# A mixture-of-experts layer on one core: three weight buffers become one ring of 20 slots

## The reference

```python
def moe_ffn(h, w_router, b_router, w_gate_up, b_gate_up, w_down, b_down):
    logits = (h @ w_router + b_router).astype(jnp.float32)
    top_v, top_e = lax.top_k(logits, TOP_K)                    # TOP_K = 4
    gate = jax.nn.softmax(top_v, axis=-1)
    ...                                                        # tokens sorted by expert, in blocks
    def expert_block(args):
        xblk, e = args
        gu = xblk @ w_gate_up[e] + b_gate_up[e]                # w_gate_up[e]: 1024 x 2048
        g = jnp.minimum(gu[:, :D_FF], SWIGLU_LIMIT)
        u = jnp.clip(gu[:, D_FF:], -SWIGLU_LIMIT, SWIGLU_LIMIT)
        hid = g * jax.nn.sigmoid(SWIGLU_ALPHA * g) * (u + 1.0)
        return hid @ w_down[e] + b_down[e]                     # w_down[e]: 1024 x 1024
    ...                                                        # weighted by gate, added per token
```

## Time and profile before

| | |
|---|---|
| timed runs, median | 1397.04 us |
| profiled execution | 1398.15 us |
| its span | 1396.1 us |
| TensorE busy (matmul) | 1076.9 us, 77% |
| TensorE weight load busy | 511.5 us, 37% |
| DVE / ACT / GpSimd busy | 426.2 / 222.2 / 117.9 us |
| moved by DMA | 472.35 MB, mean 338 GB/s |

### The profile page before, as it was taken

How to read it: one execution, slowest core, us unless ns; L and a number is a source line. 1 busy time by engine, 2 the same in 40 slices (tenths; PEclk the granted TensorE clock), 3 DMA queues, 4 the chain that set the end, 5 groups by cost and what they waited for, 6 DMA issues and landing times.

```text
span 1396.1 us, 25367 instructions
## 1 busy us (share of the span) xinstructions
PE 1076.9 (77%) x10234; PEld 511.5 (37%) x10235; DVE 426.2 (31%) x989; ACT 222.2 (16%) x428; POOL 117.9 (8%) x46
## 2 busy tenths in 40 slices
PE   3599999978796668666988997997666589666875
PEld 1367677764332223112433342342221134212322
DVE  1596787953221112111322221221111123111214
ACT  2121132113111011000121211121100011100112
POOL 0154334600000000000000000000000000000001
PEclk9899999985989889888999999999878899887987
DMA  9887956618899999999669989819999994999991
GB/s 314 260 312 249 337 213 196 247 69 354 338 417 417 419 418 418 419 416 417 288 259 417 418 348 379 342 48 418 418 418 419 418 384 170 418 418 419 416 417 71
DMA packets 111142, 472.35 MB, mean 338 GB/s; under 512 B 10736, under 2 KB 14448, under 8 KB 78224
## 3 DMA queue, kind: packets, MB, share of 16 engines
q1 hardware_dynamic: 108832, 469.03, 84.1%
q10 hardware_dynamic: 2288, 3.02, 0.9%
HBM read 470.98 MB, written 1.05 MB: 338 GB/s over the span
## 4 chain that ended last, share of the span: by engine, by line
PE 40%; DMA 36%; SPq 15%; DVE 4%; issue 3%; ACT 1%; POOL 0%; ACTq 0%; DVEq 0%
DMA down<-in_w_down_dram 17%; DMA gate_up<-in_w_gate_up_dram 16%; PE bank L1567 13%; PE bank L1234 9%; SPq L355 8%; PE bank L1602 8%; SPq L348 4%; PE bank L1537 3%; PE bank L1523 2%; DVE gate_up_r L721 2%; DMA gate_up<-in_w_ada_dram 2%; DMA gate_up<-in_w_in_dram 1%; PE bank L1256 1%; DMA gate_up<-in_w_o_b_dram 1%; ACT mod L695 1%
## 5 line engine op out<-in xcount | busy, mean ns | idle before, releaser
L1567 PE MATMUL bank<-gate_up,mod 128*32 128x512 f32 x3200 | 448.5, 692 | 204.6 <-DMA gate_up<-in_w_gate_up_dram 194.2
L1567 PEld LDWEIGHTS bank<-gate_up,mod 128*32 128x32 f32 x3200 | 102.4, 120 | 466.9 <-DMA gate_up<-in_w_gate_up_dram 289.7
L1165 DVE TENSOR_SCALAR front<-bank 128x256 f32<-128x256 f32 x50 | 21.2, 424 | 749.5 <-PE bank L1567 749.5
L1602 PE MATMUL bank<-down,mod 128*32 128x256 f32 x3200 | 190.1, 381 | 38.7 <-DMA down<-in_w_down_dram 31.0
L1234 PE MATMUL bank<-gate_up_r 128*128 128x512 f32 (+1 forms) x544 | 137.6, 400 | 20.3 <-DVE gate_up_r L721 12.6
L1602 PEld LDWEIGHTS bank<-down,mod 128*32 128x32 f32 x3200 | 98.4, 110 | 118.2 <-DMA down<-in_w_down_dram 47.4
L320 POOL TENSOR_TENSOR gate_up_r<-gate_up,gate_up_r 128x2048 fp32r<-128x2048 f32 (+1 forms) x17 | 108.7, 6397 | 127.4 <-DVE gate_up_r L721 127.4
L1234 PEld LDWEIGHTS bank<-gate_up_r 128*128 128x128 f32 x544 | 101.4, 194 | 49.1 <-issue 21.3
L692 ACT ACTIVATE front<-front 128x256 f32<-128x256 f32 x50 | 20.8, 416 | 592.4 <-DVE front L1165 592.4
L506 POOL TENSOR_TENSOR gate_up<-x_sb,gate_up 128x1024 f32<-128x1024 f32 x2 | 4.7, 2348 | 1071.2 <-DVE x_sb L1188 1071.2
L1234 PE MATMUL bank<-gate_up_r,down_r 128*128 128x512 f32 (+1 forms) x272 | 67.3, 391 | 0.0
(11 more groups left out here) (249 smaller groups left out, 727.0 us busy)
## 6 DMA issues: line engine op xcount, KB each, us to landing
gate_up<-in_w_gate_up_dram SPq DMA_DIRECT2D x128, 2048.0 KB, 24.1
down<-in_w_down_dram SPq DMA_DIRECT2D x128, 1024.0 KB, 23.4
gate_up<-in_w_ada_dram SPq DMA_DIRECT2D x12, 2048.0 KB, 9.4
gate_up<-in_w_in_dram SPq DMA_DIRECT2D x10, 2048.0 KB, 14.6
gate_up<-in_w_o_a_dram SPq DMA_DIRECT2D x2, 2048.0 KB, 7.8
gate_up<-in_w_o_b_dram SPq DMA_DIRECT2D x2, 2048.0 KB, 10.4
gate_up<-in_w_out_dram SPq DMA_DIRECT2D x2, 2048.0 KB, 7.7
gt<-in_b_in_dram SPq DMA_DIRECT2D x10, 256.0 KB, 13.3
```

What stands on the lines that cost most here:

```text
L1567: last = pe.matmul(banks[4][q * BM:(q + 1) * BM, :], xT[:, k % KG, k // KG, :], both, start=(k == 0), stop=(k == KC - 1), skip_group_check ...
L1602: last = pe.matmul(banks[7][q * BM:(q + 1) * BM, 0:HW], hidT[:, k % KG, k // KG, :], down[:, k, q * HW:(q + 1) * HW], start=(k == 0), stop ...
```

## The change

All expert weights go through one ring of 20 slots of 8 KB per partition (1 MB each), made of the same 20 MB: slots 0 to 7 are `gate_up0`, 8 to 15 `gate_up1`, and each of 16 to 19 is two chunks of `down`. An expert is 12 pieces in the order of use: 8 of gate-up (one chunk of 1 MB each, before two chunks of 2 MB) and 4 of down (two chunks, 1 MB, as before). Piece number n of the whole stream goes to slot n mod 20. Each slot has one semaphore, and TensorE waits for each piece by itself. `gu_used` now counts each of the 8 chunks. With 12 pieces an expert and 20 slots the pattern repeats after 5 experts, so the loops of SP and of TensorE have 5 bodies unrolled; TensorE has two more bodies behind its loop for experts 30 and 31. `table` gets one row more, as the counts of `gu_used` and `down_used` now differ. The diff, cut to its core:

```diff
+SLOTS = 20
+PIECES = 12
+TURN = 5
...
+        def store(slot):
+            if slot < 2 * KC:
+                return gate_up[slot // KC][:, slot % KC, :]
+            at = 2 * (slot - 2 * KC)
+            return down[:, at:at + 2, :].rearrange("p a n -> p (a n)")
...
+        def load_gate_up(eng, e, at, k):
+            eng.dma_start(store(at % SLOTS),
+                          w_gu_view[:, bass.ds(e, 1), k, :].rearrange("p a n -> p (a n)"))\
+               .then_inc(slot_in[at % SLOTS], 16)
...
             item_used(sp, "ob1")
-            first_gate_up(1, ring_slot("ob1")[0])
-            first_down(1)
-            first_down(3)
+            first_loads(ring_slots("ob1"))
+            first_loads((17, 19))
             item_used(sp, "out1")
-            for i in range(3):
-                first_gate_up(0, i)
+            first_loads(range(6))
             sp.wait_ge(ev("h2_ready"), TILES)
-            first_down(2)
+            first_loads((18,))
             z_wait(sp, "logit_parts")
-            first_down(0)
+            first_loads((16,))
             for name in ("out0", "out1"):
-                first_gate_up(1, ring_slot(name)[0])
+                first_loads(ring_slots(name))
...
-            with sp.Fori(1, E // 2) as p:
-                for s in range(2):
-                    e = p * 2 + s
-                    pieces = last_pieces(sp, bass.ds(p * 2 + (s - 2 + GMAX + 2 * E), 1))
-                    load_down(sp, p * 2 + (s - 1), pieces)
-                    load_gate_up(sp, e, s, pieces)
+            def next_down(gate_up_used, e, at):
+                for i in range(4):
+                    sp.wait_ge(ev("gu_used"), gate_up_used + i)
+                    load_down(sp, e, at + KC + i, i)
+
+            with sp.Fori(0, (E - 2) // TURN) as p:
+                for s in range(TURN):
+                    e = p * TURN + (s + 2)
+                    gate_up_used, down_used = last_pieces(sp, p * TURN + s)
+                    next_down(gate_up_used, p * TURN + (s + 1), PIECES * (s + 1))
+                    for k in range(KC):
+                        if k < 4:
+                            sp.wait_ge(ev("gu_used"), gate_up_used + (k + 4))
+                        else:
+                            sp.wait_ge(ev("down_used"), down_used + (k - 4))
+                        load_gate_up(sp, e, PIECES * (s + 2) + k, k)
...
-            with pe.Fori(0, E // 2) as p:
-                for s in range(2):
+            def expert(e, s, turns):
+                def piece(i):
+                    at = PIECES * s + i
+                    pe.wait_ge(slot_in[at % SLOTS], turns * 16 + (16 * (at // SLOTS) + 16))
+                    return store(at % SLOTS).rearrange("p (a n) -> p a n", a=2)
...
+                    for k in range(KC):
+                        w = piece(k)
...
+            turns = PIECES * TURN // SLOTS
+            with pe.Fori(0, E // TURN) as p:
+                for s in range(TURN):
+                    expert(p * TURN + s, s, p * turns)
+            for s in range(E % TURN):
+                expert(E // TURN * TURN + s, s, E // TURN * turns)
```

More of the change, by code:

```diff
@@ L221, in bass_hybrid_layer @@
         assert at[0] <= 4 * D - FF // 2
-        table = sb("table", [1, GMAX + 3 * E + 4], I32)
+        table = sb("table", [1, GMAX + 4 * E + 4], I32)
+        GU_AT, DOWN_AT, TOTAL_AT = GMAX + 2 * E, GMAX + 3 * E, GMAX + 4 * E
         sm = sb("sm", [P, 320])
@@ L267, in bass_hybrid_layer @@
         t_free = [sem(f"t_free{i}") for i in range(2)]
-        gu_in = [[sem(f"gu_in{s}_{i}") for i in range(4)] for s in range(2)]
-        dn_in = [sem(f"dn_in{i}") for i in range(4)]
+        slot_in = [sem(f"slot_in{i}") for i in range(SLOTS)]
         evs = {}
@@ L339, in last_pieces, with load_down, first_load @@
         def last_pieces(eng, at):
[L340 to L357, removed]
+            return [eng.value_load(table[0:1, bass.ds(at + first, 1)], min_val=1, max_val=KC * GMAX)
+                    for first in (GU_AT, DOWN_AT)]
+        def load_gate_up(eng, e, at, k):
+            eng.dma_start(store(at % SLOTS),
+                          w_gu_view[:, bass.ds(e, 1), k, :].rearrange("p a n -> p (a n)"))\
+               .then_inc(slot_in[at % SLOTS], 16)
+        def load_down(eng, e, at, i):
+            eng.dma_start(store(at % SLOTS).rearrange("p (a n) -> p a n", a=2),
+                          w_dn_view[:, bass.ds(e, 1), 2 * i:2 * i + 2, :].rearrange("p a k n -> p (a k) n"))\
+               .then_inc(slot_in[at % SLOTS], 16)
+        def first_load(eng, slot):
+            e, i = slot // PIECES, slot % PIECES
+            if i < KC:
+                load_gate_up(eng, e, slot, i)
+            else:
+                load_down(eng, e, slot, i - KC)
         b_ada_rows = b_ada[0].rearrange("(j q n) -> q j n", j=12, q=NQT)
@@ new lines, in expert @@
+            def expert(e, s, turns):
[3 more added lines that the diff above has]
+                    return store(at % SLOTS).rearrange("p (a n) -> p a n", a=2)
+                first = pe.value_load(table[0:1, bass.ds(e + (GMAX + E), 1)], min_val=0, max_val=GMAX - 1)
+                blocks = pe.value_load(table[0:1, bass.ds(e + GMAX, 1)], min_val=1, max_val=S // BM)
+                with pe.Fori(0, blocks) as b:
+                    g = first + b
+                    pe.wait_ge(ev("xT_ready"), g + 1)
+                    pe.wait_ge(ev("hot_ready"), g + 1)
+                    for k in range(KC):
+                        w = piece(k)
+                        for q in range(NG):
+                            last = pe.matmul(banks[4][q * BM:(q + 1) * BM, :], xT[:, k % KG, k // KG, :],
+                                             w[:, :, q * HW:(q + 1) * HW],
+                                             start=(k == 0), stop=(k == KC - 1), skip_group_check=True)
+                        last.then_inc(ev("gu_used"), 1)
+                        if k == 0:
+                            for a in range(2):
+                                for q in range(NG):
+                                    pe.matmul(banks[4][q * BM:(q + 1) * BM, a * HW:(a + 1) * HW], onehot,
+                                              bias_parts[a][:, q * HW:(q + 1) * HW], start=False, stop=False,
+                                              skip_group_check=True)
+                    pe.wait_ge(ev("y_ready"), g + 1)
+                    pe.wait_ge(ev("gT_ready"), g + 1)
+                    combine()
+                    pe.wait_ge(ev("sel_ready"), g + 2)
+                    gather()
+                    pe.wait_ge(ev("selg_ready"), g + 1)
+                    for t in range(TILES):
+                        last = pe.transpose(banks[5][:, t * P:(t + 1) * P], selg[:, t, :], ident[:, :])
+                    last.then_inc(ev("gt_done"), 1)
+                    pe.wait_ge(ev("hid_ready"), g + 1)
+                    for i in range(KG):
+                        last = pe.transpose(banks[7][:, i * P:(i + 1) * P], hid[:, i * P:(i + 1) * P], ident[:, :])
+                    last.then_inc(ev("ht_done"), 1)
+                    pe.wait_ge(ev("xe_ready"), g + 2)
+                    gather_T()
+                    pe.wait_ge(ev("hidT_ready"), g + 1)
+                    for i in range(KC // 2):
+                        w = piece(KC + i)
+                        for k in (2 * i, 2 * i + 1):
@@ L1607, in _ @@
-            total = pe.value_load(table[0:1, GMAX + 3 * E:GMAX + 3 * E + 1], min_val=1, max_val=GMAX - 1)
+                        last.then_inc(ev("down_used"), 1)
+            turns = PIECES * TURN // SLOTS
[4 more added lines that the diff above has]
+                expert(E // TURN * TURN + s, s, E // TURN * turns)
+            total = pe.value_load(table[0:1, TOTAL_AT:TOTAL_AT + 1], min_val=1, max_val=GMAX - 1)
```

44 lines of the change are left out of this document (22 added, 22 removed).

## The result

| | before | changed | forecast |
|---|---|---|---|
| median | 1397.37 us (4 runs) | 1365.88 us (1363.81 to 1368.24, 4 runs) | 1348 (1341 to 1359) |
| ratio | | 0.9774, 95% interval 0.9761 to 0.9786 | 0.965 |
| profiled execution (span) | 1398.15 (1396.1) | 1366.62 (1364.6) | 1349.0 |

The account below looks back on a forecast made before the run. The loop was taken as bound by the weight stream's busy time plus its stops. 51.1 us gained, less 1.5 for pieces and 0.5 for the unrolled loop, made 49.1 us: 1348 us, range 1341 to 1359.

Parts of the forecast that it names:

- (a) to (c): Weight stream: room unchanged, so stops begin as before but end 10.4 us earlier; over five stops 51.1 us gained.
- early restart: Next down weights wait for the last block's first gate-up piece, not first down piece; a stop ends 10.4 us earlier.
- (d): TensorE from 713.30 to 940.14 us: 23.5 us of waits can absorb 18.5 us from two stops, 5 us to spare.
- (e): Twice as many gate-up transfers, 1 MB instead of 2: cost between nothing and 7 us, 1.5 us taken.
- (f): TensorE's waits, 12 a block for 8: hidden by the matmuls, 0; without cover 8 us at most.
- (g): TensorE's loop unrolled over 5 experts, not 2: rarer wraps gain below 1 us; 0.5 us of cost taken.
- rival 3: Five-body loop not held, TensorE's code fetched again every pass behind the weights: about 620 us slower; chance 0.04.
- stops two and four: Weight-stream stops at experts 11 and 17: idle 23.5 and 36.4 us before, 13.1 and 26.0 us forecast to stay.
- stop three: Weight-stream stop at expert 15: idle 8.1 us before, less than the 10.4 us gained, so forecast to go.
- (h): First fill, with expert 0's down pieces after its gate-up pieces: cost 0, 2 us at most.
- (i): Tail: the last gate-up pieces are finer, but the last down piece ends later than they do; 0.

Follow-up runs that it names:

- two rings without the hint: The changed kernel, 1365.88 us, and the same kernel with the next down pieces waiting for down_used of the last block, 1417.25 us.
- the two with it: The changed kernel and its version with down pieces waiting for down_used, each with a prefetch hint for TensorE's jump back: 1347.46 and 1401.43 us.
- 18 slots: Changed kernel with a ring of 18 slots instead of 20, so TensorE's loop has 3 bodies: 1374.26 us.
- hinted ring: Changed kernel with a prefetch hint for the jump back of TensorE's loop, nothing else: 1350.6 us, timed again 1347.46 us.
- unrolled kernel: Changed kernel with TensorE's 32 expert bodies written out, no loop over experts, block counts read at fixed places of `table`: 1356.31 us.
- late ones: Changed kernel with next down pieces waiting for down_used of the last block, not gu_used: 1417.25 us; with a prefetch hint for TensorE's jump back 1401.43 us.
- head aligned: Changed kernel with the first instruction of TensorE's 5-body loop at the start of a block of 256 instructions: 1364.06 us.
- loop of 8 bodies: Kernel before, old buffers, TensorE's loop unrolled over 8 experts instead of 2: 1408.49 us; with a prefetch hint for the jump back 1410.56 us.

## Why the prediction was wrong, point by point

- **(a) to (c), the stops, right.** Forecast were 51.1 us for the early restart; measured are 51.4 between the two rings without the hint, 1401.4 - 1347.5 = 54.0 between the two with it. That the first comes so close is in part luck, as the stalls and packets are in both of its kernels and need not cost the same; the second has neither. The room sets where a stop begins (18 slots), the first gate-up piece where it ends.
- **(d), TensorE can follow, right in itself**: in the hinted ring the stop at expert 15 is gone. In the changed kernel it is not, because one of the 7 us stalls, that ahead of expert 15, falls into this stretch, the one that I had called the tightest point of the sum and given 5 us to spare. The unrolled kernel, with the packets but no stall, has no stop there either (414 GB/s from 816 to 824).
- **(e) and (f), pieces and waits**: 1.5 us taken, nothing found; the lower bound was right.
- **(g), the unrolled loop, is the step that failed.** It was put at 0.5 us and measured 15 to 18 (1365.88 - 1350.6 = 15.3, 1365.88 - 1347.46 = 18.4, and 19.9 - 3.1 = 16.8 between the late ones). Fetching the loop again costs twice, by a stall and by its packets. Two errors are in it. The first is the row it rested on: 15 packets show that two bodies are held, and nothing of five; the bounds of a resource that the trace does not show had to be wide, and rival 3, where they were, got 4% and only as an extreme. "Runtime: NRT & Kernel Launch", section "Instruction fetch mechanics", in the Trainium skill, warned of just this: a taken branch to a place that is not held waits for a fetch before execution goes on. The runs agree, with 6.7 to 7.6 us at each such jump. Its figure of 2048 instructions for TensorE I read as room for five bodies; unhinted they were not held, hinted they were, and 8 were not either way.
- The second error is the sentence on stalls in rival 3: "A stall at the six wraps alone, even 10 us each, lies inside the 15 us and costs next to nothing." (There are six passes and so five jumps back.) It holds where TensorE is tied to the stream, and by the table above that is so for four of the five. It fails for expert 15, where (d) of the same prediction left TensorE 5 us and not 15. The hinted ring's waits for weights between stops two and four add up to 5.6 us, as (d) has it, but only 0.70 us of them (at 791.66) lie between the jump at expert 15 and the place of stop three. So the stall there brings stop three back, idle for 5.8 us, and costs about 7.
- The changed kernel's profile has 3.9 us more at stop two, and the stall at expert 10 does not explain them: with the head aligned the same stall, 6.46 us, leaves 0.2. By 658 TensorE waits for weights again (1.47 and 1.67 us before the last two down pieces of expert 11's first block):

```profile
661.39 1.93 PE L1627 MATMUL bank<-gate_up,mod 128*32 128x256 f32 x16 [1.67 <-DMA gate_up<-in_w_down_dram]
663.09 1.94 PE L1592 MATMUL bank<-gate_up,mod 128*32 128x512 f32 x8
...
675.49 3.66 PE L1627 MATMUL bank<-gate_up,mod 128*32 128x256 f32 x64 [0.15 <-ACT mod L715]
```

The same place in the hinted ring:

```profile
658.48 1.07 PE L1627 MATMUL bank<-gate_up,mod 128*32 128x256 f32 x16 [1.48 <-DMA gate_up<-in_w_down_dram]
659.36 1.04 PE L1592 MATMUL bank<-gate_up,mod 128*32 128x512 f32 x8
...
669.84 3.44 PE L1627 MATMUL bank<-gate_up,mod 128*32 128x256 f32 x60
```

The last piece is used 2.9 us later, although until 658 the two streams ran at 416 and 417 GB/s. Then the changed kernel runs at the lower of TensorE's two clocks, in 661 to 667 us at a granted clock of 0.50, behind these waits, where 658 to 664 us of the hinted ring have 1.00:

```profile
661.00:667.00 6.00, 5.61 (x44) 1.98 (x48) 0.00 (x0) 1.67 (x2) 0.00 (x0) 0.50 1.01 419
```

```profile
658.00:664.00 6.00, 5.53 (x68) 2.18 (x72) 0.00 (x0) 1.67 (x2) 0.00 (x0) 1.00 1.01 422
```

That is 0.8 us in the 16 down records and 1.9 us in the block behind them (12.4 us from gate-up to down for 10.5). With the 2.9 us it makes the 5.65 us by which SP's issue is later, 694.17 for 688.52. In the head-aligned and the unrolled kernel the piece is used at 660.51 and 660.41, and at the higher clock (1.07 us).
- **Why pieces land later is argued, not shown.** In all six kernels with 57 packets or more the stream fades over some 6 us at stop two; in those with 15 to 22 it ends within 2 to 4. Windows of 2 us, changed kernel:

```profile
674.00:676.00 2.00, 1.85 (x26) 0.98 (x22) 0.88 (x3) 0.77 (x2) 0.00 (x0) 1.00 0.96 397
676.00:678.00 2.00, 2.00 (x44) 1.27 (x40) 1.18 (x6) 0.00 (x0) 0.00 (x0) 1.00 0.60 250
678.00:680.00 2.00, 2.00 (x40) 0.99 (x35) 0.13 (x1) 0.77 (x2) 0.00 (x0) 1.00 0.41 172
680.00:682.00 2.00, 2.00 (x29) 0.71 (x24) 0.00 (x0) 0.90 (x1) 0.00 (x0) 1.00 0.07 29
```

the unrolled one (57 packets, no stalls):

```profile
674.00:676.00 2.00, 2.00 (x36) 0.92 (x32) 0.42 (x2) 0.55 (x2) 0.00 (x0) 1.00 0.76 315
676.00:678.00 2.00, 2.00 (x32) 0.76 (x28) 0.00 (x0) 1.12 (x1) 0.00 (x0) 1.00 0.51 213
678.00:680.00 2.00, 2.00 (x24) 0.63 (x20) 0.00 (x0) 0.00 (x0) 0.00 (x0) 1.00 0.10 41
```

and the kernel before:

```profile
684.00:686.00 2.00, 2.00 (x32) 0.74 (x24) 0.00 (x0) 1.66 (x2) 0.00 (x0) 1.00 1.00 418
686.00:688.00 2.00, 2.00 (x24) 0.68 (x20) 0.00 (x0) 0.01 (x1) 0.00 (x0) 1.00 0.53 217
688.00:690.00 2.00, 2.00 (x24) 0.67 (x20) 0.00 (x0) 0.00 (x0) 0.00 (x0) 1.00 0.01 4
```

So the fading goes with the packets and not with the stalls. It would fit 16 DMA engines of which some have fallen behind under the instruction packets, a piece being complete only with its slowest engine; the trace does not show single engines, so that stays an explanation. By the unrolled kernel the packets are worth 5.7 to 8.9 us.
- **Stops alone do not close the account.** 102.4 - 65.6 = 36.8 us less idle, 31.5 us gained. The last wait for weights moved from 1364.22 to 1332.77 (table above), by 31.5, so the 5.3 us lie ahead of it. Most of them can be found. Summed over slices of 6 us from 320 us to the last wait, the idle time is 106.5 us before and 70.8 changed, 35.7 less, and in that stretch the changed kernel moves 1.5 MB more (393.4 for 391.9 MB), 0.85 MB of it instructions; at 418 GB/s that is 3.7 us. What is left is 32.0 us, the gain within 0.5. The same account for the hinted ring gives 106.5 - 54.5 - 2.0 = 50.0 us, and its last wait moved by 50.4.
- **(h) and (i)**: the first down weights were not waited for, and the tail behind the last wait is 31.8 us where it was 31.9. Right.
- **Rival 3** named the mechanism and its sign, but its price was worked out for packets behind the whole stream, 24.1 us each, and for 31 experts. Measured are one stall of about 7 us at each of five jumps, of which one counts; that did not make the kernel slower than before.

## What to carry to other kernels

When a stream is the bound, list its stops and ask for each what begins and what ends it: a buffer layout is worth what it moves the end, and here that could be read off the timeline to 6% (51.1 us for 54.0). Every extra body that a layout needs for its pattern to repeat is code: look at the instruction queue's packet count before and after, and take a jump back over more code than the trace has shown held as a stall until a run shows otherwise. A stall costs where the engine is not waiting for the stream anyway, so compare it with what is spare at its own place and not with the average. Try the prefetch hint on the jump: it is one word and was worth 15 to 18 us here, though nothing for the loop of 8 bodies.

## What the runs showed of the hardware

- TensorE loops of 2 and 4 expert bodies come with 15 and 18 instruction packets (of 16 KB: 1.10 MB in 67), so they are held; one of 5 comes with 67 packets and 6.7 to 7.6 us of idle at each jump back. In instructions that is some 730, 1460 and 1830, an estimate at 365 a body: TensorE and its weight loads execute 351 a block, and waits come on top. With the hint the same 5 bodies take 22 packets and 1.2 us at the two jumps where no weights are waited for. With 8 bodies (about 2900) hint or none make little difference: 63 and 64 packets, 6.8 to 9.1 us. Why the hint changes what is kept, not only when it is fetched, is open.
- Putting the loop's head at the start of a block of instructions did not help (68 packets, 1364.06 us).
- With 57 packets instead of 22 and no stalls the kernel takes 5.7 to 8.9 us more; how the packets cost that is open.
- Gate-up weights in 1 MB and in 2 MB transfers, both with runs of 8 KB, stream alike: 418 GB/s over 268 us.
